# Residual in tiles, an early weight stream and bias rows in twelve stores, in a two-block transformer kernel

## The reference, cut to what matters

```python
x = x + g_a * (concatenate([y_m, y_a]) @ w_out[l])            # "mix"
x = x + g_f * conv_glu(modulate(rmsnorm(x, ...)), w_up, ..., w_down)   # ends in "down1"
# second block
xn = rmsnorm_2(x, attn_norm_g[l])
proj = xn @ w_in[l]
y_pool = pool_mixer(u_pool, pool_w[l], pool_scale[l])
y_dil = dilated_attention(qkv_dil, rel_bias)                   # s + bias[...] before the softmax
y_sb = stick_breaking_attention(qkv_sb)
y_s5 = s5_mixer(u_s5, ...)
x = x + merged @ w_out[l]                                      # "out2"
x = x + (silu(gu[..., :FFN]) * gu[..., FFN:]) @ w_down[l]      # "down2"
return rmsnorm_2(x, final_norm_g)
```

## Time and profile before

| | |
|---|---|
| runs shown | 4195.84 us median, 4190.08 to 4208.63 |
| the profiled execution | 4197.49 us, its span 4195.6 us |
| PE busy | 3685.7 us, 88% of the span |
| PEld (weight loads, beside PE) | 2954.8 us, 70% |
| DVE / ACT / POOL busy | 1439.9 / 1052.0 / 854.6 us |
| DMA | 304.39 MB, mean 73 GB/s |

### The profile page before, as it was taken

One profiled execution on the slowest core, in us unless ns is written; L12 is line 12 of the kernel. 1 busy time (PEld: TensorE's weight loads), 2 busy tenths in 40 slices (PEclk: granted clock), 3 DMA queues, 4 the chain that ended last, 5 costly groups with the idle time before them and its releaser, 6 DMA issues. The chain is left out here.

```text
span 4195.6 us, 46232 instructions
## 1 busy us (share of the span) xinstructions
PE 3685.7 (88%) x17523; PEld 2954.8 (70%) x17523; DVE 1439.9 (34%) x2084; ACT 1052.0 (25%) x1875; POOL 854.6 (20%) x680
## 2 busy tenths in 40 slices
PE   4689979977999979966999895789999779999898
PEld 3467768765888867844888674477777668888676
DVE  5244553454322334432324442134443330000343
ACT  3423421133111122310222351033333320000232
POOL 3110033111333300022222453001111113333000
PEclk7798989988999989988999997799999889999999
DMA  7610021122111122312111114222222321111322
GB/s 231 204 29 21 9 59 28 42 101 90 50 40 50 50 97 83 101 53 47 43 50 60 29 31 106 54 87 91 90 92 93 118 91 50 50 50 30 130 91 80
DMA packets 288681, 304.39 MB, mean 73 GB/s; under 512 B 28858, under 2 KB 234842, under 8 KB 287238
## 3 DMA queue, kind: packets, MB, share of 16 engines
q1 hardware_dynamic: 285880, 292.34, 22.4%
q10 hardware_dynamic: 2270, 9.25, 1.0%
q0 software_dynamic: 384, 0.81, 0.1%
HBM read 261.03 MB, written 40.67 MB: 72 GB/s over the span
## 5 line engine op out<-in xcount | busy, mean ns | idle before, releaser
L172 PE MATMUL ps<-h_hi_at,w_hi 128*128 128x512 f32 x1408 | 549.7, 390 | 46.2 <-POOLq L202 46.2
L172 PE MATMUL ps<-h_lo_at,w_hi 128*128 128x512 f32 x1408 | 549.3, 390 | 0.0
L172 PE MATMUL ps<-h_hi_at,w_lo 128*128 128x512 f32 x1408 | 549.0, 390 | 0.0
L172 PEld LDWEIGHTS ps<-h_hi_at,w_hi 128*128 128x128 f32 x1408 | 265.2, 188 | 102.8 <-POOLq L202 47.8
L2247 PE MATMUL ps<-xn_hi_at,w_hi 128*128 128x512 f32 x608 | 250.5, 412 | 87.8 <-POOL w_lo L2212 49.3
L172 PEld LDWEIGHTS ps<-h_lo_at,w_hi 128*128 128x128 f32 x1408 | 265.3, 188 | 55.3
L172 PEld LDWEIGHTS ps<-h_hi_at,w_lo 128*128 128x128 f32 x1408 | 265.2, 188 | 55.3
L2247 PE MATMUL ps<-xn_hi_at,w_lo 128*128 128x512 f32 x608 | 247.8, 408 | 0.0
L2247 PE MATMUL ps<-xn_lo_at,w_hi 128*128 128x512 f32 x608 | 247.2, 406 | 0.0
L200 POOL CAST w_hi<-xT 128x1024 fp32r<-128x1024 f32 x88 | 91.5, 1040 | 752.9 <-POOLq L63 752.9
L1653 PE MATMUL ps<-down_s_hi,down_w_hi 128*128 128x512 f32 x704 | 183.6, 399 | 49.4 <-ACT down_s_hi L1477 42.5
(11 more groups left out here) (518 smaller groups left out, 6744.2 us busy)
## 6 DMA issues: line engine op xcount, KB each, us to landing
xT<-in_w_up SPq DMA_DIRECT2D x88, 512.0 KB, 5.0
down_raw<-in_w_down SPq DMA_DIRECT2D x88, 512.0 KB, 3.2
mg_raw<-in_w_gate SPq DMA_DIRECT2D x128, 256.0 KB, 2.6
wa<-in_w_ada SPq DMA_DIRECT2D x24, 1024.0 KB, 7.9
raw<-in_w_in SPq DMA_DIRECT2D x76, 256.0 KB, 2.9
mg_raw<-in_w_branch SPq DMA_DIRECT2D x56, 256.0 KB, 2.5
xT<-x_saved SPq DMA_DIRECT2D x3, 4096.0 KB, 12.6
stream_raw<-in_w_in SPq DMA_DIRECT2D x44, 256.0 KB, 2.8
```

The lines of the kernel that those rows point to most:

```text
L172: last = nc.tensor.matmul(bank_of(s, part, n)[:, 0:size], w[:, k, :], r[:, k, at:at + size], start=(k == 0 and j == 0), stop=(k == k_tiles ...
```

## The change

Five edits are made.

1. In all four products the residual is loaded in eight transfers of 512 KB, each issued behind one of the first eight weight tiles.
2. In `down1` SP and GpSimd begin the branches' stream: SP issues its first four weight loads ahead of the two stores of the sum, and GpSimd splits the first two. The stream's buffers get an address of their own. The wait for the stores moves to the front of SP's side work in the next block, and the separate end of stage between the two goes.
3. GpSimd makes the rests of tiles 1, 3 and 5 of the second half, in `down1` (tile 7 goes back to VectorE) and now in `mix` and `out2` too; in `mix` it first adds the shift.
4. The bias rows are stored by twelve transfers of 192 KB, one head of one group each, two ahead of each of the six pooling slots, with a semaphore for each group.
5. In `s5_branch` the matmuls of an even and an odd group alternate.

```diff
+BRANCH_AT = 214976
...
-        product_norm(c, "down1", ..., save=(xT, saved[1]), other=range(16, 21))
-        c.end_stage()
-        second_block(c, io, xT, ident, ones, gains, s5, xn, hid, h, saved)
+        branches = Stream(c, "px", branch_jobs(io), xn[0], xn[1], 2, None, at=BRANCH_AT)
+        ahead = product_norm(c, "down1", ..., save=(xT, saved[1]), other=range(16, 21), ahead=branches)
+        second_block(c, io, xT, ident, ones, gains, s5, xn, hid, h, saved, branches, ahead)
...
+    begun, by_pool = [], (1, 3, 5) if h is not None else ()
...
-            sp.dma_start(first[0][:, :, :], first[1]).then_inc(first_loaded, 16)
             for u in range(2 * K):
                 if u >= 2:
                     sp.wait_ge(lo_made, u - 1)
                 sp.dma_start(raw[:, u % 2, :], w[:, u % K, :]).then_inc(loaded[u % 2], 16)
+                if u < DK:
+                    sp.dma_start(first[0][:, u, :], first[1][:, u, :]).then_inc(first_loaded, 16)
+            if ahead is not None:
+                begun.append(ahead.sp(sp))
+                next(begun[0])
...
-            if saves:
+            if saves and ahead is None:
                 sp.wait_ge(saved, 32)
...
-                    if k and h is not None and (half == 0 or k % 2 or outer is None):
+                    if k and h is not None and (half == 0 or k - 1 not in by_pool):
                         rest(half, k - 1)
...
+            if ahead is not None:
+                begun.append(ahead.pool(pool))
+                next(begun[1])
+            for k in by_pool:
+                pool.wait_ge(rounded, DK + k + 1)
+                plain = h[2][:, k, part(1)]
+                if shift is not None:
+                    step(nc.gpsimd.tensor_scalar(plain, plain, shift(k), None, ALU.add))
+                nc.gpsimd.tensor_tensor(h[1][:, k, part(1)], plain, h[0][:, k, part(1)].bitcast(F32), ALU.subtract).then_inc(rest_made, 1)
...
-        for g in ORDER:
-            act.dma_start(skewed[g], off[:, g, :].unsqueeze(1).to_broadcast([DH, P, SKEW])).then_inc(skew_stored, 16)
...
+        pieces = [(n, h) for n in range(3) for h in range(DH)]
         for s in range(N_POOL):
+            for n, h in pieces[2 * s:2 * s + 2]:
+                act.dma_start(skewed[ORDER[n], h:h + 1], off[h:h + 1, ORDER[n], :].unsqueeze(1).to_broadcast([1, P, SKEW])).then_inc(skew_stored[n], 16)
...
+            sp.wait_ge(skew_stored[n], 16 * DH)
...
+        sp.wait_ge(ahead[2], 32)
         sp.dma_start(rel, io["rel_bias_2"]).then_inc(set_loaded, 16)
...
-                for g in range(8):
-                    q, rows = g // 2, slice(64 * (g % 2), 64 * (g % 2) + 64)
...
+                for q in range(4):
+                    pair = [(2 * q + gg, slice(64 * gg, 64 * gg + 64), c.ps[:, 4 + 2 * (m % 2) + gg, q * P:(q + 1) * P]) for gg in range(2)]
+                    for g, rows, dst in pair:
+                        nc.tensor.matmul(dst, toep[:, m % 2, g, :], chunk[:, 8 * m + g, :], start=True, stop=False)
                     for j in range(2):
+                        for g, rows, dst in pair:
+                            last = nc.tensor.matmul(dst[:, 1:P], cp[rows, m % 2, j, q, 1:POW, :].rearrange("p d ch -> p (d ch)"),
+                                                    state[rows, m % 2, j, q, 0:S5_N - 1], start=False, stop=(j == 1))
```

More of the change, by code:

```diff
@@ L1424, in split_pair, with product_norm @@
     return [c.sb(f"{name}_{n}", shape, ctx, F32R) for n in ("hi", "lo")]
-def product_norm(c, name, w, k_tiles, src, x, gate, first, bufs, h, gain, shift=None, outer=None, save=None, other=None):
+def product_norm(c, name, w, k_tiles, src, x, gate, first, bufs, h, gain, shift=None, outer=None, save=None, other=None, ahead=None):
     nc = c.nc
@@ L1689, in _ @@
             last.then_inc(mean_ready, 1)
+    return begun + [saved]
 def product_buffers(c, name, at):
@@ L2059, with second_block @@
 S5_N = T // S5_L
-def second_block(c, io, xT, ident, ones, gains, s5, xn_pair, hid, h, saved):
+def second_block(c, io, xT, ident, ones, gains, s5, xn_pair, hid, h, saved, branches, ahead):
     nc = c.nc
@@ L2070, in second_block @@
             with ExitStack() as s2:
-                pool_and_dilated(c, io, w_in, xn_hi, xn_lo, yT, xT, ident, s2)
+                pool_and_dilated(c, io, branches, ahead, yT, xT, ident, s2)
             c.end_stage()
@@ L2321, in spread, with branch_jobs, pool_and_dilated @@
     return order + [True] * (n_stream - taken)
-def pool_and_dilated(c, io, w_in, xn_hi, xn_lo, yT, spare, ident, s2):
+DIL_ORDER = (1, 2, 0)
+def branch_jobs(io):
+    w_in = io["w_in_2"][0].rearrange("(k p) n -> p k n", p=P)
+    job = lambda at, turned: [w_in[:, :, at:at + P], None, turned, None]
+    jobs = [job(O_POOL + g * P, None) for g in range(len(POOLS))]
+    for g in DIL_ORDER:
+        at = O_DIL + g * 256
+        jobs += [job(col, None) for col in (at, at + P, at + 768, at + 768 + P)] + [job(at + 1536 + m * P, True) for m in range(2)]
+    return jobs + [job(O_SB + 1024 + h * P, True) for h in range(4)] + [job(O_SB + h * P, None) for h in (0, 1, 4, 5)]
+def pool_and_dilated(c, io, st, ahead, yT, spare, ident, s2):
     nc = c.nc
@@ L2397, in tokens_to, with skew_kept, wrapped @@
         return place
-    jobs = [(cols(O_POOL + g * P), to_tile(u[:, g, :]), None, None) for g in range(G)]
+    def skew_kept(fn):
+        def wrapped(eng, *rest):
+            for sem in skew_stored:
+                eng.wait_ge(sem, 16 * DH)
+            return fn(eng, *rest)
+        return wrapped
+    jobs = [(to_tile(u[:, g, :]), None, None) for g in range(G)]
     qk_job, v_job = [], []
     for n, g in enumerate(ORDER):
-        at = O_DIL + g * 256
         qk_job.append(len(jobs))
-        for m, col_at in enumerate((at, at + P, at + 768, at + 768 + P)):
+        for m in range(4):
             put = to_tile(qk_of[n][:, m, :])
-            jobs.append((cols(col_at), (put, after(skew_stored, 48, put), after_group(0, put))[n], None, None))
+            jobs.append(((put, skew_kept(put), after_group(0, put))[n], None, None))
         v_job.append(len(jobs))
@@ L2748, in _ @@
         def _(sp):
-            woven(order, st.sp(sp), side_sp(sp))
+            woven(order, ahead[0], side_sp(sp))
         @block.gpsimd
         def _(pool):
-            for _ in st.pool(pool):
+            for _ in ahead[1]:
                 pass
```

51 lines of the change are left out of this document (23 added, 28 removed).

## The result

The changed kernel takes 4093.2 us (median of four runs, 4085.0 to 4097.7), the kernel before 4201.6 us in the same session: a ratio of 0.975, 95% interval 0.973 to 0.977. The forecast was 4140 us with a range from 4098; the time fell out of it on the fast side. The profiled execution took 4094.6 us, its span is 4092.7 us, 102.9 us less than before.

A forecast was written before the change was run, and what follows sets the result against it. TensorE, busy 88% of the span, was taken as the bound, so only its idle places could gain. Terms -41 - 15.3 + 0 - 3 + 3 = -56 us gave 4140 us; own range 4122 to 4160, 8-in-10 range 4098 to 4162.

The forecast's parts named there:

- Starts: Starts of the four products: residual in tiles lets first weights land sooner, 61.8 to 20.4 us, a gain of 41 us.
- third rival: Products behind the four starts: two transfers to a unit slow the weights and eat the 41 us; about 4180 us, chance 0.07.
- Early stream: From `down1` to the branches: first two units already split, so TensorE starts earlier, a gain of 15.3 us.
- Bias rows: Branches: ScalarE's stall goes but a starved weight queue takes its place; 0, with +15 or -39 us possible.
- source limit: Bias stores: the source partitions, not the engines, limit the rate; twelve stores at about 26.7 GB/s, 88 us together.
- q10 and q1 take turns packet by packet: Bias stores: one packet of the weight queue passes per bias packet, each turn now costing 0.89 us on every engine.
- forecast stall of 36 us: Branches: TensorE waits for weight loads held behind bias packets, 36 us in sum.
- first rival: Bias stores run free on all 16 engines, about 1 us each; -39 us, giving 4101 us, chance 0.19.
- S5 halves: `s5_branch`: 64-row matmuls alternating row halves run faster, 0.14 against 0.18 us each; -3 us, from 0 to -8.
- Rests on GpSimd: Ends of `mix`, `out2` and `down1`: VectorE slows while GpSimd subtracts; +3 us, from -2 to +7.

The follow-up runs named there:

- e7: The changed kernel with the residual again loaded by one transfer of 4 MB ahead of the weights; 4136.7 us.
- e4: The changed kernel with each bias row lying 32 times over in partitions, its twelve stores each reading 32 partitions; 4079.2 us.
- e8: The changed kernel with the rests of `mix` and `out2` back on VectorE, GpSimd making them only in `down1`; 4088.8 us.
- e3: The changed kernel with three bias stores on four engines, as before, but one ahead of each of pooling slots 0, 2 and 4; 4105.0 us.
- e5: The changed kernel with the S5 outputs in the old order, one group after the other; 4100.9 us.
- e2: The changed kernel with its twelve bias stores all issued at the old place, ahead of the pooling slots; 4139.4 us.
- e1: The changed kernel with the bias rows stored as before, three stores of 512 rows at the old place; 4128.0 us.
- e14: The changed kernel with each bias store of 128 rows cut in two of 64 whole rows, 24 stores on sixteen engines; 4089.5 us.

## Why the prediction was wrong

- **Starts, -41**: right. 61.8 - 21.5 = 40.3 us, and e7 gives 43. The third rival (paid back) is false.
- **Early stream, -15.3**: right, 15.1 us. (VectorE's end is 1825.7 in the forecast's own rows and 1825.4 in its sum, a slip of 0.3 us.) The stores' landing was late next for SP, as said, and cost nothing.
- **Bias rows, 0**: wrong, and the term that decides. It was -40. The source limit, on which it stood, is real: 26 GB/s from one partition with sixteen engines. So is "q10 and q1 take turns packet by packet", inside a store: 54 beside 54. What failed is the next step, "a weight load had 32 packets on each slowed engine, one per bias packet", taken over to the new shape as 32 turns of 0.89 us, 28 us for a load. It supposes that a bias packet always stands ready. That held where a store had 128 packets on an engine; it has 8 now, and at its end the rest of the load passes. A load waits for one store, 8 packets or 7.2 us, and not for 32 packets or 28 us; TensorE took a load every 6.5 us there anyway (e4), so that the forecast stall of 36 us was 7 us (2.7 for `px_w_lo`, 4.3 for a copy). The sum of the stall has a slip as well: 28 + 2 us where 20 are free is 10, not 12. And 26.7 GB/s was the rate of an engine that reads whole tiles, put in for that of a partition; that the measured 26 to 27 GB/s is nearly the same is luck. The first rival had the right size, -39, for the wrong reason: its stores should have run in 1 us each, and they took about 7.
- **S5 halves, -3**: the mechanism was right, the size was not: -14.6. The price came from 16 matmuls in 2.25 us, 0.14 each. That row is of a group whose operands lie every fourth column. The same line, further on in the kernel before, has adjacent columns:

```profile
2224.47 1.16 PE L2470 MATMUL ps<-dil_even 64*128 64x128 f32 x16
```

  0.073 us each. With this row 128 matmuls save 0.105 us each, and the half of them that ran at the low clock twice that: 20 us. The four rounds lost 18.9 us (47.6 to 28.7), of which the stretch kept 14.6. The number was in the trace, on the line that I read, in its last group. But the agreement is in part luck: the term names only the halves, and some two fifths of the gain are the fewer changes between 128-row and 64-row matmuls, which it put at nothing.
- **Rests on GpSimd, +3**: right, +4.3, undone by e8.
- **Not forecast**: `mix`'s product took 2.5 us more in the changed profile, with a granted clock of 0.75 in its first 12 us (0.87 before) and 0.96 to 0.95 between 929 and 969. e3, e5 and e8 have the same loads and take 93.1, 93.0 and 93.2 us there, while e2 and e4 take 95.6 and 96.0. So the same code gives either, and the 2.5 us aren't a fixed price of the change; what decides between the two isn't shown.

The forecast's -56.3 with 39.6 more from the branches and 11.6 from S5, less 1.3 for the rests, 2.5 for `mix` and 0.9 for the starts and the junction, gives -102.8, which is what the profiled spans differ by (102.9). The medians differ by 108; the openings explain such a gap, but which part of it they are isn't shown.

## What to carry to other kernels

A small source that is stored many times over should be spread over partitions that lie on different ports before anything is done about engines, pieces or spacing. Turns of one to one between two queues say how long a load waits only as long as the other queue has packets on that engine: count how many of one transfer lie there before you carry the rule to another shape. When a duration is taken from a row of the same kind, look at all rows of that line and at the stride of their operands first. When an experiment changes the order of matmuls, count how often their row count changes too.

## What the hardware showed beyond expectation

- The same bytes in more transfers hold the issuing engine longer: 43.4 us for three (e1, at 24 GB/s), 70.9 us for twelve (e2, at 27 GB/s). In e14 a store of 96 KB takes 3.6 us of the queue but lands 14.4 us after issue: about four transfers are under way when the next issue is held. In e1 the third is held with two under way, so it isn't a plain count of four; the rule isn't shown.
- Two 64-row matmuls on different row halves pass TensorE together: eight take 0.71 us, as long as four on the same rows. On the same rows one more costs 0.11 us at the high clock, with or without a change of bank. Each run of them between 128-row matmuls costs 0.39 us more, so few long runs are better than many short ones. The Trainium skill, "TensorEngine Tiling (Array Packing)", section "Tiling Modes", lists 64x128 as two tiles; the trace agrees.
- Four rows in partitions 0 to 3, in 0, 32, 64, 96 and in 0, 36, 72, 108 leave at 24, 48 and 90 GB/s through four engines.
